# Three seven-product pairs of steps in each SwiGLU layer, two of them side by side

## What is computed

```python
D_MODEL = 1024; SEQ = 256; DEPTH = 2; D_FF = 2816

def swiglu(x, w_in, w_out):
    gate, up = jnp.split(x @ w_in, 2, axis=-1)
    return (jax.nn.silu(gate) * up) @ w_out

for i in range(DEPTH):
    h = layer_norm(DN_ALPHA * h + 0.5 * swiglu(h, ffn_w_in[i, 0], ffn_w_out[i, 0]), ...)
    m = gla_mixer(h, ...) if i % 3 == 0 else retention_mixer(h, ...)
    h = layer_norm(DN_ALPHA * h + m, ...)
    h = layer_norm(DN_ALPHA * h + 0.5 * swiglu(h, ffn_w_in[i, 1], ffn_w_out[i, 1]), ...)
# then one attention block with a squared-ReLU layer
```

## Time and profile before

| | |
|---|---|
| median of 3 runs | 1499.16 us (1499.13 to 1499.2) |
| the profiled execution | 1499.28 us, its span 1497.5 us |
| TensorE (PE) busy | 1487.8 us, 99% |
| VectorE (DVE) busy | 1074.1 us, 72% |
| ScalarE (ACT) busy | 814.6 us, 54% |
| GpSimd (POOL) busy | 143.3 us, 10% |

### The profile page before, as it was taken

One profiled execution on the slowest core, in us unless ns is written; L12 is line 12 of the kernel. 1 busy time (PEld: TensorE's weight loads), 2 busy tenths in 40 slices (PEclk: granted clock), 3 DMA queues, 4 the chain that ended last, 5 costly groups with the idle time before them and its releaser, 6 DMA issues.

```text
span 1497.5 us, 18806 instructions
## 1 busy us (share of the span) xinstructions
PE 1487.8 (99%) x7798; PEld 1268.6 (85%) x7798; DVE 1074.1 (72%) x1115; ACT 814.6 (54%) x827; POOL 143.3 (10%) x144
## 2 busy tenths in 40 slices
PE   9999999999999999999999999999999999999998
PEld 8888888888888888888888888888998888888886
DVE  7698677777868688677566768866786466775555
ACT  6465566556556565553434556555645666354443
POOL 0020010200002000024031200002002200020000
PEclk9999999999999999999999999999999999999999
DMA  9773654576657656555544675655444434465551
GB/s 393 255 260 106 246 208 169 204 263 218 218 193 289 228 188 194 207 219 195 177 165 169 257 261 186 195 205 220 169 152 176 152 141 147 162 228 193 197 195 58
DMA packets 45444, 301.71 MB, mean 201 GB/s; under 512 B 5440, under 2 KB 5888, under 8 KB 10672
## 3 DMA queue, kind: packets, MB, share of 16 engines
q1 hardware_dynamic: 38592, 270.35, 48.2%
q0 software_dynamic: 4960, 26.41, 7.5%
q10 hardware_dynamic: 1808, 3.74, 0.7%
HBM read 282.60 MB, written 1.05 MB: 189 GB/s over the span
## 4 chain that ended last, share of the span: by engine, by line
PE 98%; DMA 1%; SPq 0%; issue 0%; ACT 0%; DVE 0%; POOLq 0%; POOL 0%; DVEq 0%
PE psum L2000 16%; PE psum L2003 16%; PE psum L2004 16%; PE psum L2109 13%; PE psum L2113 7%; PE psum L2136 6%; PE psum L2246 3%; PE psum L2247 3%; PE psum L2250 3%; PE psum L2143 3%; PE psum L2032 2%; PE psum L2045 2%; PE psum L2038 2%; PE psum L2012 1%; DMA weights_raw_more<-in_weights 1%; PE psum L2267 0%
## 5 line engine op out<-in xcount | busy, mean ns | idle before, releaser
L1180 DVE TENSOR_TENSOR weights_lo<-weights_raw,weights_hi 128x2048 fp32r<-128x2048 f32 x187 | 431.6, 2312 | 219.6 <-ACT weights_hi L609 218.1
L609 ACT ACTIVATE weights_hi<-weights_raw 128x2048 fp32r<-128x2048 f32 x194 | 364.3, 1882 | 222.7 <-PE psum L2004 136.2
L2000 PE MATMUL psum<-weights_hi,hidden_hi 128*128 128x512 f32 x416 | 163.3, 393 | 0.0
L2003 PE MATMUL psum<-weights_lo,hidden_hi 128*128 128x512 f32 x416 | 162.5, 391 | 0.0
L2004 PE MATMUL psum<-weights_hi,hidden_lo 128*128 128x512 f32 x416 | 162.0, 389 | 0.0
L2000 PE MATMUL psum<-weights_hi,operand 128*128 128x512 f32 x384 | 151.5, 394 | 0.0
L2003 PE MATMUL psum<-weights_lo,operand 128*128 128x512 f32 x384 | 149.9, 390 | 0.0
L2109 PE MATMUL psum<-operand,weights_hi 128*128 128x512 f32 x608 | 144.6, 390 | 0.0
L2004 PE MATMUL psum<-weights_hi,operand 128*128 128x512 f32 x352 | 137.2, 390 | 0.0
L2109 PEld LDWEIGHTS psum<-operand,weights_hi 128*128 128x128 f32 x608 | 112.9, 188 | 22.7
L1180 DVE TENSOR_TENSOR weights_lo<-weights_raw_more,weights_hi 128x2048 fp32r<-128x2048 f32 x52 | 117.8, 2286 | 4.0 <-ACT weights_hi L609 4.0
(11 more groups left out here) (379 smaller groups left out, 2690.5 us busy)
## 6 DMA issues: line engine op xcount, KB each, us to landing
weights_raw<-in_weights SPq DMA_DIRECT2D x194, 1024.0 KB, 4.8
weights_raw_more<-in_weights SPq DMA_DIRECT2D x60, 1024.0 KB, 8.0
weights_raw<-weights_raw_more POOLq DMA_DIRECT2D x8, 1024.0 KB, 11.0
weights_raw<-weights_raw POOLq DMA_DIRECT2D x8, 1024.0 KB, 6.9
ln_rows<-in_ln_rows POOLq DMA_DIRECT2D x16, 512.0 KB, 7.6
weights_raw<-in_weights SPq DMA_DIRECT2D x4, 256.0 KB, 4.0
weights_raw<-in_weights SPq DMA_DIRECT2D x2, 512.0 KB, 5.9
normalised<-in_x POOLq DMA_DIRECT2D x2, 512.0 KB, 12.9
```

Source lines behind the costliest of these rows:

```text
L609: nc.scalar.activation(hi[:, rest], whole[:, rest], ACT.Copy).then_inc(hi_split, 1)
L1180: nc.vector.tensor_tensor(lo_of(n), raw_of(n), hi_of(n).bitcast(F32), ALU.subtract).then_inc(lo_split, 1)
L2000: mm(out, a_hi, b_hi, start=start, stop=False, skip_group_check=True)
L2003: mm(out, a_hi, b_lo, start=False, stop=False, skip_group_check=True)
```

## The change

`GROUPS` goes from (5, 8) to (3, 5, 8). Steps 3 and 4, plain before, become a pair, followed at once by the pair of steps 5 and 6. The planner's tables, lengths and counts follow from `GROUPS`. In the first layer ScalarE's split of the fifth operand moves behind the first `silu`. At step 2 VectorE splits T1 of the pair behind the two gate/up sums instead of ahead of them.

```diff
-GROUPS = (5, 8)
+GROUPS = (3,5,8,)
@@ ScalarE, ffn()
-                split_hi(n0 + 4)
+                if f:
+                    split_hi(n0 + 4)
                 silu(n0, pairs[0][:, :, 0:TOK])
+                if not f:
+                    split_hi(n0 + 4)
@@ VectorE, summed_step()
                     if after in GROUPS:
+                        if j == 2:
+                            split_lo(n0 + GROUP_AT[after] + 1)
                         add_t2(after)
@@ VectorE, ffn()
-                        if after in GROUPS:
+                        if after in GROUPS and j > 2:
                             split_lo(ahead + 1)
```

## The result

The changed kernel takes 1513.5 us (median of 4 runs, 1513.1 to 1515.2) against 1499.1 for the kernel before (4 runs, 1499.05 to 1499.2): the ratio is 1.0097, with a 95% interval of 1.0085 to 1.0109. It is slower by 14.4 us, at the predicted time.

The account below looks back on a forecast made before the run. TensorE, busy 99% of the span, was taken to bound the kernel. Layers 2 to 4 at +1.4 us each and the first at +10.0, added to 1499.28, gave 1513.5, forecast as 1513, range 1494 to 1520.

Parts of the forecast that it names:

- The pair saves 2.3 us: Steps 3 and 4 as a pair take 30.8 us instead of 33.2: 2.3 us less in each of four layers.
- The pair at step 3 costs nothing in layers 2 to 4: VectorE's operands and T1 arrive in time for the added pair at step 3; no stall there.
- T1 of step 5 is late, and everything hangs on it: Pair at step 5: load waits for a buffer freed at 11.0 us; T1 DMA takes 13.6, landing at 30.0.
- The deadline of 26.3: D1 of the pair at step 5 is in time if T1 lands within 26.3 us of step 3's pair start.
- The stall of 3.7 us: Pair at step 5: TensorE waits 1.7 at P3, 1.2 at P5, 0.8 at D1; layers 2 to 4 net +1.4 each.
- The first layer: First layer is worse by three places: 3.8 + 2.0 + 6.5 - 2.3 = +10.0 us.
- The third place: First layer, pair at step 5: T1 queued behind layer-norm rows and constants, landing 34.8; costs 6.5 us, bounds 2 and 8.
- The sum: Whole kernel: 1499.28 + 3 x 1.4 + 10.0 = 1513.5 us.
- Early: Rival, chance 0.16: step 5's T1 DMA takes 8.3 us, landing at 24.7 before the deadline; 1490 to 1495 us.
- Worse: Rival, chance 0.07: late pair makes step 8's T1 late too, 2 to 3 us a layer; 1522 us or so.
- GpSimd's residual operations in the first layer's pair at step 3: Two VectorE operations run slow beside them (3.13 instead of 2.28 us); cost 2.0 us, bounds 0 and 3.

Follow-up runs that it names:

- e1: Changed kernel without the T1 DMA of the pair at step 5, in all four layers; 1495.8 us, ratio 0.9973.
- e9: Changed kernel, SyncE holding loads from b22 on until step 5's T1 is made, later ScalarE split in first layer only, GpSimd's second T1 earlier there; 1492.5 us.
- e10: As e9, but with the changed kernel's ScalarE order and the first layer's load ("up", 3, 1) held until T1 of step 3 has landed; 1493.0 us.
- e3: Changed kernel with GROUPS = (3, 8): two pairs a layer with plain steps between; 1504.4 us, ratio 1.0032.
- e6: Changed kernel, ScalarE splitting step 3's T1 behind copies and silu in all layers, GpSimd issuing the first layer's second T1 earlier; 1516.7 us, ratio 1.0112.
- e4: Changed kernel, SyncE holding loads from ("down", 3) on until T1 of step 5 has landed; 1505.7 us, ratio 1.0040.
- e5: As e4, but holding from two loads earlier, ("up", 5, 1); 1501.0 us, ratio 1.0011.
- e2: Changed kernel with GROUPS = (5, 7): two pairs a layer side by side, none at step 3; 1502.5 us, ratio 1.0017.
- e7: Changed kernel with the edits of e5 and e6 together; 1501.8 us, ratio 1.0014.
- e8: Changed kernel with nine unused matmuls on TensorE ahead of P3's low half in the pair at step 5; 1514.7 us, ratio 1.0100.

## Why the prediction was right

- **The pair saves 2.3 us.** Right: layers 3 and 4 of e1, and 2 to 4 of e9 and e10, save 2.3 or 2.4.
- **The pair at step 3 costs nothing in layers 2 to 4.** Right: 30.84 us in the second, no wait; e3 shows it alone. The cover is thin: e6 moved one ScalarE operation and lost 1.9 to 2.5 us a layer, and a T1 of 15.1 us (e1, second layer) lost 0.6.
- **T1 of step 5 is late, and everything hangs on it.** Right, and shown by taking it away (e1) and by making it land sooner (e4, e5, e9). Issue was forecast at T = 16.4 and is at 16.8 in the second layer; the DMA at 13.6 and is 13.5, 14.2 and 13.8 in layers 2 to 4; the landing at 30.0 and is at 30.4.
- **The deadline of 26.3.** Right: landings at 22.9 (e2) and 25.2 (e9) cost nothing, one at 28.5 (e4) cost 2.4.
- **The stall of 3.7 us** was sized too low by 0.7. The third layer's three idle times add up to 3.63, but each restart costs more than its idle time: by the starts of matmuls (554.72, then 557.30; the normal distance is 0.23) the first is 2.35, not 2.20, and the four low-half matmuls behind it take 1.04 instead of 0.91. So counted, the three make 4.4, 0.5 of which is T1 landing at T = 30.5. Layers 2 to 4 therefore grew by 1.9, 2.2 and 1.9, not by 1.4.
- **The first layer** was forecast at 3.8 + 2.0 + 6.5 - 2.3 = +10.0 and grew by 7.7. The down tile waited 3.7, with T1 landing at 42.9 (43.8 forecast). In the pair at step 3 the two waits make it 32.96 us long (48.97 to 81.93), 2.1 us over. The third place was mis-sized: T1 was issued at T = 21.2 as forecast, but its DMA took 11.7 us, not 13.6, and the pair at step 5 took 117.49 - 81.93 = 35.56 us, 4.7 over and not 6.5. The wait of 3.7 cost 4.0 by the starts of matmuls. And 0.9 us was gained ahead of all this: TensorE's 1.30 us wait at 23.17 of the kernel before, in the opening, for the first hidden values, is not there after. The prediction had put the split that moves behind the first `silu` at nothing; the rows show `silu` 1.7 us earlier by it, which ends the wait. No run has this edit alone. Timelines of PE and ACT of the kernel before, then of ACT after:

```profile
23.17 0.66 PE L2221 MATMUL psum<-constants,hidden 128*128 128x128 f32 x4 [1.30 <-DVE hidden L1299]
...
21.80 0.60 ACT L661 ACTIVATE silu_gate<-psum 128x512 f32<-128x512 f32 x1
...
20.10 0.60 ACT L661 ACTIVATE silu_gate<-psum 128x512 f32<-128x512 f32 x1
```

- **The sum.** Predicted +10.0 + 4.2 = 14.2, measured 7.7 + 6.0 = 13.7, and 0.6 at the end of the span. The stalls of layers 2 to 4 came out larger and the first layer smaller, and the two nearly cancel: that the time is so close is in part luck.
- **The rivals.** "Early" was not far off: in layers 2 to 4 of e2, e5 and e9 the DMA of the late T1 took 6.8 to 9.0 us, by the placing of a load or two. "Worse" did not come: the pair at step 8 had no wait.
- **GpSimd's residual operations in the first layer's pair at step 3.** Sized at 2.0 us, measured 2.1, and the rows bear the cause out: two VectorE operations beside them took 1.7 us longer together, as forecast. P5's low half was ready 1.0 us after TensorE wanted it, so without the 1.7 it would have been in time (an estimate). In e1 the two operations are as slow, and the waits are gone by the lower clock, not by T1. e9 and e10 have waits at the same places (1.4 and 0.5 or 0.6) with the residual operations later and both VectorE operations at 2.28 or 2.29; there VectorE is late from the start of the pair, in e9 because ScalarE's split of T1 comes later, in e10 because b22 does. No run moved the residual operations alone.

## What to carry to other kernels

A buffer's free time fixes when a transfer can start, so when two stages are moved side by side, work out for each transfer the time from the release of its buffer to the deadline of the chain behind it, and compare that with its slow duration, not the median. If it is late, look at which other loads are in flight from a few us before it, and hold back those that are wanted last; holding one that is wanted soon moves the wait (e5, e10), unless it is the first to go out afterwards and lands in time (b22 in e9). Count stalls by the starts of matmuls, not by idle times.

## What the runs showed of the hardware

The accumulating DMA for T1 of the second pair of two side by side, 1 MB, took 6.8 to 9.0 us in layers 2 to 4 where no load had been issued in the last 3 us before it (e2, e5, e7, e9, e10), and 11.5 to 14.3 where one had been issued 0.5 to 1.0 us before it (the changed kernel, e4, e6, e8). Loads issued only before it (e4, 11.5 to 12.1) cost nearly as much as a stream on both sides. This is no full rule: the first T1 of layers 2 to 4 took 13.4, 9.9 and 13.9 us in the changed kernel, with one load 1.1 to 1.6 us before it.

A full-tile VectorE operation took 3.12 or 3.13 us instead of 2.28 beside GpSimd's residual operations, in the changed kernel, e1 and e3.

The granted clock fell from 1.00 to 0.50 with waits of 2.0 and 2.3 us in layers 1 and 2, and not with waits of 2.2 in the third layer or 3.7 at 46.12 us, of the same execution. At that first down tile the changed kernel, e1, e3, e4, e5 and e8 waited 3.7 to 4.6 us; the clock fell in all but the changed kernel, in e1, e4 and e5 before the wait had ended, and in e5 it was at 0.50 until about 52 us. Of the nine waits of 1.8 to 2.3 us in the pairs of the changed kernel, e2 and e6, four were followed by a drop. What decides between a drop and none is open; that idling comes before it is shown by e8, where the filled waits had none.
